# Two chained transformer blocks in fp32 on one core: block borders, the final layer norm and the first slots of each layer in a new order

## The reference, cut to what matters

```python
# first block, one layer (first_block)
hn = rms_norm(h, ln_pre_mix)
# projections, sliding-window and forgetting attention -> mix
h = h + rms_norm(mix @ w_out, ln_post_mix)
hn = rms_norm(h, ln_pre_ffn)
gu = hn @ w_gate_up                           # 1024 -> 2 * 2816
ff = (silu(gu[..., :D_FF]) * gu[..., D_FF:]) @ w_down
h = h + rms_norm(ff, ln_post_ffn)
# second block, two layers (hybrid_layer)
shift, scale, gate = split(silu(c) @ w_ada + b_ada)
u = x * (1 + scale) + shift
proj = u @ w_in                               # conv, gates, latents of q and kv, merge logits
# three branches, one of them latent attention -> m
x = layer_norm(DEEPNORM_ALPHA * x + gate * (m @ w_o), ln_g, ln_b)
```

## Time and profile before

| | us |
|---|---|
| median of 3 runs | 2003.44 (2001.84 to 2005.49) |
| the profiled execution's own time | 1998.23 |
| its span, first to last instruction | 1996.4 |
| TensorE busy with matmuls | 1818.6 |
| VectorE busy | 1068.3 |
| ScalarE busy | 703.0 |
| GpSimd busy | 129.9 |
| mean granted TensorE clock | 0.958 of full speed |

### The profile page before, as it was taken

The page is one execution under the profiler, slowest core; times in us unless marked ns, Lnnn a source line. Parts: engine busy times, 40 slices in busy tenths (PEclk is TensorE's granted clock), DMA queues, the critical chain, the costliest instruction groups (busy, mean ns, idle before and its releaser), DMA issues.

```text
span 1996.4 us, 20299 instructions
## 1 busy us (share of the span) xinstructions
PE 1818.6 (91%) x8139; PEld 1416.4 (71%) x8139; DVE 1068.3 (54%) x1694; ACT 703.0 (35%) x1131; POOL 129.9 (7%) x129
## 2 busy tenths in 40 slices
PE   4999999889999998989999999994889999999993
PEld 3765555568888787767778788773667778788772
DVE  6144444286666325563447867553453448866453
ACT  3324444342221223245532322423255532322422
POOL 1100000101010001000000000013000000000012
PEclk9899999799999999999989999997899999999996
DMA  3311000225555322121113222221121112232210
GB/s 131 131 66 41 22 22 22 74 95 211 180 209 183 114 104 106 63 85 64 64 43 104 86 94 96 85 92 56 64 85 64 64 43 105 85 106 85 98 71 42
DMA packets 29100, 177.40 MB, mean 89 GB/s; under 512 B 3565, under 2 KB 3709, under 8 KB 11726
## 3 DMA queue, kind: packets, MB, share of 16 engines
q1 hardware_dynamic: 20016, 144.71, 20.3%
q0 software_dynamic: 8608, 31.21, 4.6%
q10 hardware_dynamic: 382, 0.19, 0.1%
HBM read 171.28 MB, written 4.78 MB: 88 GB/s over the span
## 4 chain that ended last, share of the span: by engine, by line
PE 67%; DVE 7%; ACT 3%; POOL 1%; issue 1%; DMA 1%; POOLq 0%; ACTq 0%; DVEq 0%
PE ps L553 21%; PE ps L555 20%; PE ps L554 20%; PE ps L1006 2%; DVE w_lo L1462 2%; PE ps L991 2%; DVE R L1507 1%; ACT h L1053 1%; POOL acc L472 1%; ACT w_hi L1053 1%; PE ps L997 1%; PE ps L593 1%; DVE cacc L1469 0%; DMA w_raw<-in_w 0%; DVE ps L1824 0%
## 5 line engine op out<-in xcount | busy, mean ns | idle before, releaser
L553 PE MATMUL ps<-Xh,w_hi 128*128 128x512 f32 x1616 | 652.3, 404 | 55.7 <-DVE Xl L1462 26.2
L555 PE MATMUL ps<-Xh,w_lo 128*128 128x512 f32 x1616 | 636.5, 394 | 0.0
L554 PE MATMUL ps<-Xl,w_hi 128*128 128x512 f32 x1616 | 636.3, 394 | 0.0
L1462 DVE TENSOR_TENSOR w_lo<-w_raw,w_hi 128x2048 fp32r<-128x2048 f32 (+1 forms) x152 | 313.6, 2063 | 339.7 <-ACT w_hi L1053 339.7
L553 PEld LDWEIGHTS ps<-Xh,w_hi 128*128 128x128 f32 x1616 | 308.0, 191 | 132.7 <-issue 42.5
L1053 ACT ACTIVATE w_hi<-w_raw 128x2048 fp32r<-128x2048 f32 (+1 forms) x152 | 259.4, 1707 | 314.4 <-DMA w_raw<-in_w 282.5
L554 PEld LDWEIGHTS ps<-Xl,w_hi 128*128 128x128 f32 x1616 | 308.6, 191 | 65.9 <-issue 4.6
L555 PEld LDWEIGHTS ps<-Xh,w_lo 128*128 128x128 f32 x1616 | 307.7, 190 | 66.2
L1469 DVE SCALAR_TENSOR_TENSOR cacc<-ain,vec,cacc 128x512 f32<-128x512 f32 x240 | 161.9, 746 | 0.0
L1053 ACT ACTIVATE gt<-ps 128x512 f32<-128x512 f32 x48 | 28.2, 597 | 201.2 <-PE ps L555 201.1
L553 PE MATMUL ps<-act_h,w_hi 128*128 128x512 f32 x176 | 70.9, 403 | 4.3 <-DVE act_l L1462 4.3
(11 more groups left out here) (296 smaller groups left out, 2250.0 us busy)
## 6 DMA issues: line engine op xcount, KB each, us to landing
w_raw<-in_w SPq DMA_DIRECT2D x134, 1024.0 KB, 4.8
ada_w<-in_w_ada POOLq DMA_DIRECT2D x48, 512.0 KB, 4.6
bias_scratch<-brow POOLq DMA_DIRECT2D x2, 1312.0 KB, 5.3
h<-in_xT SPq DMA_DIRECT2D x4, 512.0 KB, 6.2
out<-h SPq DMA_DIRECT2D x1, 2048.0 KB, 6.3
bias<-bias_scratch POOLq DMA_DIRECT2D x1, 1024.0 KB, 7.6
bias<-bias_scratch POOLq DMA_DIRECT2D x1, 512.0 KB, 4.9
cact<-in_c POOLq DMA_DIRECT2D x1, 512.0 KB, 6.6
```

The source lines that it names most:

```text
L553: nc.tensor.matmul(o_, whi, xhi, start=start, stop=False)
L554: nc.tensor.matmul(o_, whi, xlo, start=False, stop=False)
L555: return nc.tensor.matmul(o_, wlo, xhi, start=False, stop=stop)
L1462: return nc.vector.tensor_tensor(o_, a_, b_, op)
```

## The change

Out projection: the first two tiles of slot 11 are computed together, k outermost (`window_step`), the first half of them ahead of the last attention values. Gate/up: `sums(2)` and the 128x512 reciprocal give way to `token_sums` and `spread` inside the last k-step of `two_slots`; ScalarE copies the spread result to `R`. `two_slots` waits for the second slot's `w_lo` by quarters. Down: the first four activation tiles are split during the last two gate/up slots, the output tiles are taken in another order at first with a wait for each bank, and the four late adaptive columns move between the down slots. End of down: VectorE adds the squares, ScalarE and VectorE share the copies to `y`, and the split of slot 47 is cut in quarters. Layer start: other banks, `sums(nsum)` between the two tiles of slot 2, slot 4's `slot_hi` ahead of the fifth latent and its `slot_lo` ahead of the latents. Layer end: after four of the eight output tiles their mean (of 512 channels) is taken off all 8 tiles of `h`; the true mean's difference to it (`delta`) and the variance are 128x4 sums at the end. Layer 1's input is made tile by tile with `lnp` (gain and bias merged with scale and shift); `h` itself stays without gain and bias, and the scaling by DEEPNORM_ALPHA in layer 1 adds them. The result is stored in four parts of 512 KB.

The diff, cut to its core, with eight columns of indentation less:

```diff
+EARLY = KD // 2
...
+LAT_BANK = (2, 3, 4, 5, 0, 6)
...
-    sp.wait_ge(ln_out, LAYERS * KD)
-    sp.dma_start(out, h[:, :, :]).then_inc(out_done, 16)
-    sp.wait_ge(out_done, 16)
+    for i in range(4):
+        sp.wait_ge(ln_out, 2 * i + 2)
+        sp.dma_start(out[:, 2 * i:2 * i + 2, :], h[:, 2 * i:2 * i + 2, :]).then_inc(out_done, 16)
...
-    add_early_squares(1, 1)
+    add_up(KD, 1, squares(0, KD - 1, KD))
+    pool.wait_ge(sum_full, 2)
+    pool.sem_inc(sq_added, 1)
...
-    add_early_squares(3, 2)
...
-        add_up(n + (5 + 2 * KC + KD), norm + 5, squares(0, KD, nsq + (5 + KC)))
+                for j in range(EARLY)])
+        add_up(n + (5 + 2 * KC + EARLY), norm + 5, squares(0, KD - 1, nsq + (5 + KC)))
+        pool.wait_ge(sum_full, norm + 6)
+        pool.sem_inc(sq_added, 1)
...
-    def two_slots(g, ready):
-        pe.wait_ge(w_lo_done, g + 2)
...
+        split_ready(g)
         for k in range(KD):
             pe.wait_ge(lo_done, ready + k + 1)
+            if norm is not None and k == KD - 1:
+                token_sums(norm, (norm + 1) * KD, (), B_ST)
             for i in range(4):
+                if i == 2:
+                    split_ready(g + 1, k // 2)
+                if norm is not None and k == KD - 1 and i == 3:
+                    spread(norm, B_O)
                 whi, wlo = w(g + i // 2, k * 2 * P + i % 2 * P)
-                last = mm3(bank(i), whi, wlo, Xh[:, k, :], Xl[:, k, :], k == 0, k == KD - 1)
+                last = mm3(bank(b0 + i), whi, wlo, Xh[:, k, :], Xl[:, k, :], k == 0, k == KD - 1)
...
+    def window_step(k):
+        pe.wait_ge(o_lo, 4 + k + 1)
+        for j in range(2):
...
+        if u == UNITS - 1:
+            split_ready(S_OW)
+            window_step(0)
+            window_step(1)
         values(u)
     assert done == DENSE_STEPS
+    window_step(2)
+    window_step(3)
...
+        for j in range(2 if g == S_OW else 0, 4):
...
-    sums(2, 3 * KD)
+    two_slots(S_GU, KD, 0, norm=2)
...
+    def down_bank(j):
+        if j in (0, 2):
+            pe.wait_ge(bank_read[0], fills.f[0].val())
+        if j == 1:
+            pe.wait_ge(bank_read[1], fills.f[1].val(-1))
+        if j in (6, 3):
+            pe.wait_ge(bank_read[1], fills.f[1].val())
...
-                for j in range(KD):
+                for j in (4, 5, 7, 0, 1, 2, 6, 3):
+                    if q == 0 and kk == 0:
+                        down_bank(j)
...
-    keep_busy(3, bank(B_O), T)
+    for b in range(2):
...
+    token_sums(3, 4 * KD - 2, (KD - 2, KD - 1), 0)
+    keep_busy(1, bank(1), T)
+    spread(3, 1)
+    keep_busy(3, bank(0), T)
...
-        two_slots(G, split0)
-        sums(nsum, nadd + 3)
-        pe.wait_ge(w_lo_done, G + 3)
+        two_slots(G, split0, 2)
...
-                last = mm3(bank(4 + j), whi, wlo, Xh[:, k, :], Xl[:, k, :], k == 0, k == KD - 1)
+                last = mm3(bank(LAT_BANK[4 + j]), whi, wlo, Xh[:, k, :], Xl[:, k, :], k == 0, k == KD - 1)
             last.then_inc(tile_full if j == 0 else slot_done, 1)
+            if j == 0:
+                sums(nsum, nadd + 3)
...
+                    if s == 0 and j == 0:
+                        pe.wait_ge(lo_done, split0 + (KD + 5 + 3 * KC + k + 1))
+                    if 2 * s + j == EARLY and k == KD - 3:
+                        sums(nsum + 4, nadd + (5 + 2 * KC + EARLY))
+                    whi, wlo = w(g, k * 2 * P + j * P)
+                    last = mm3(bank(j), whi, wlo, Xh[:, k, :], Xl[:, k, :], k == 0, k == KD - 1)
+                last.then_inc(tile_full if j == 0 else slot_done, 1)
...
+        pe.wait_ge(mean_added, 2 * L + 2)
+        pe.wait_ge(bank_read[0], fills.f[0].val())
+        block_sums(0, R, True)
+        pe.wait_ge(sq_added, nadd + (5 + 2 * KC + EARLY + KD - 1))
+        pe.wait_ge(rt_done, nsum + 5)
+        block_sums(2, acc, True)
+        pe.wait_ge(bank_read[1], fills.f[1].val())
+        block_sums(0, h[:, KD - 1, :], False, True).then_inc(mean_full, 1)
+        pe.wait_ge(sq_ready, SQ1 + SQUARES2 * L + SQUARES2)
+        block_sums(2, sq[:, (KD - 1) % 2, :], False, True).then_inc(sum_full, 1)
+        for i in range(2):
+            pe.wait_ge(diag_done, SPREADS1 + 2 * L + i + 1)
+            for t in range(NB):
+                last = nc.tensor.matmul(bank(B_O + i, P, c0=P * t), ones[:, :], tmp[:, i, t * P:(t + 1) * P],
+                                        start=True, stop=True)
+            last.then_inc(r_spread, 1)
+        if L + 1 < LAYERS:
+            keep_busy(3, bank(3), T)
...
-    root(2)
+    token_root(2, B_ST)
+    sc.wait_ge(r_spread, 2)
+    act_(R[:, :], bank(B_O), ACT.Copy).then_inc(r_copied, 1)
...
+        if t >= KF - 2:
+            down_hi(t - (KF - 2))
...
+    for q in range(1, KF // 2):
+        slot_hi(S_DOWN + q + 1)
+        if q > 1:
+            down_hi(q)
...
         square(bank(j), 3 * KD + j, j)
+        if j in (0, 2, 4):
+            y_copied = act_(y[:, j, :], bank(j), ACT.Identity, scale=vec1[:, 3 * KD + j:3 * KD + j + 1])
...
-    token_root(3, 4)
+    token_root(3, 0)
+    for j in (KD - 2, KD - 1):
+        act_(y[:, j, :], bank(j), ACT.Identity, scale=vec1[:, 3 * KD + j:3 * KD + j + 1]).then_inc(down_read, 1)
...
-                next_hi(3)
+                next_hi(L_CG)
+                next_hi(L_CG + 1)
...
-        next_hi(L_CG + 1)
...
-            act_(h[:, j, :], h[:, j, :], ACT.Copy, scale=DEEPNORM_ALPHA).then_inc(h_scaled, 1)
+            if L == 0:
+                act_(h[:, j, :], h[:, j, :], ACT.Copy, scale=DEEPNORM_ALPHA).then_inc(h_scaled, 1)
+            else:
+                act_(h[:, j, :], h[:, j, :], ACT.Identity, scale=lnp[:, 2, j:j + 1], bias=lnp[:, 3, j:j + 1]
...
+        act_(warm[:, :], eps[:, 0:1], ACT.Sqrt)
...
+        def centred_square(j):
+            if j < EARLY:
+                sc.wait_ge(zc_ready, (KC + EARLY) * L + (KC + j + 1))
+            else:
+                sc.wait_ge(bank_read[j % 2], FILL1[j % 2] + FILL2 * (L + 1) - 4 + j // 2 + 1)
+            square(h[:, j, :], nadd + (5 + 2 * KC + EARLY + j), j)
...
         for j in range(KD):
-            sc.wait_ge(zc_ready, (KC + KD) * L + (KC + j + 1))
-            square(h[:, j, :], nadd + (5 + 2 * KC + KD + j), j)
-        root(nsum + 5, 1)
...
+            centred_square(j)
+        sc.wait_ge(var_done, L + 1)
+        act_(rs[:, :], var[:, :], ACT.Sqrt, bias=eps[:, 1:2]).then_inc(rt_done, 1)
+        if L + 1 == LAYERS:
+            for j in range(KD):
+                sc.wait_ge(ln_mid, KC * LAYERS + j + 1)
+                act_(h[:, j, :], h[:, j, :], ACT.Identity, scale=vec(L, V_LG + j), bias=vec(L, V_LB + j)
+                     ).then_inc(ln_out, 1)
...
-    slot_lo(S_GU + 2)
-    inv_root(2)
-    ve.wait_ge(cact_done, 1)
+    for part in range(2):
+        slot_lo(S_GU + 2, part)
+    token_roots(2)
+    for part in range(2, 4):
+        slot_lo(S_GU + 2, part)
+    ve.wait_ge(r_copied, 1)
...
+        if t >= KF - 2:
+            down_lo(t - (KF - 2))
...
+        if t == 0:
+            ve.wait_ge(cact_done, 1)
...
+    for q in range(1, KF // 2):
+        slot_lo(S_DOWN + q + 1)
+        if q > 1:
+            down_lo(q)
+        if 2 <= q < 6:
+            c = 2 * KF + q - 2
+            ada_column(c, c // 2, c % 2, sgate[:, :, :].rearrange("p a n -> p (a n)"))
...
+    ln_g, ln_b = vec2[:, 0, V_LG:V_LG + KD], vec2[:, 0, V_LB:V_LB + KD]
+    ts(lnp[:, 2, :], ln_g, DEEPNORM_ALPHA, None, ALU.mult)
+    ts(lnp[:, 3, :], ln_b, DEEPNORM_ALPHA, None, ALU.mult)
+    tt(lnp[:, 0, :], ln_g, ada[:, 32:40], ALU.mult)
+    own.link(tt(lnp[:, 1, :], ln_b, ada[:, 32:40], ALU.mult))
+    own.link(tt(lnp[:, 1, :], lnp[:, 1, :], ada[:, 24:32], ALU.add))
...
+    for j in range(1, KD - 2):
...
+            tt(acc[:, :], acc[:, :], sq[:, j % 2, :], ALU.add).then_inc(sq_added, 1)
+        if j % 2:
+            y_copied = ts(y[:, j, :], bank(j), vec1[:, 3 * KD + j:3 * KD + j + 1], None, ALU.mult)
...
+    for part in range(2):
+        slot_lo(SLOTS1 + 1, part)
+    token_roots(3)
+    ve.wait_ge(r_spread, 3)
+    ve.sem_inc(sq_added, 2)
...
-        ve.wait_ge(sq_ready, 3 * KD + j + 1)
-        ts(y[:, j, :], bank(j), vec1[:, 3 * KD + j:3 * KD + j + 1], None, ALU.mult
...
+        if j >= KD - 2:
+            ve.wait_ge(down_read, j - (KD - 3))
+        own.link(tt(tmp[:, j % 2, :], y[:, j, :], bank(1), ALU.mult))
...
+        if 1 <= j < 3:
+            slot_lo(SLOTS1 + 1, j + 1)
...
-        if L:
-            next_lo(1)
-            split_input(lambda o_, j: ts(o_, h[:, j, :], ada_col(8 + j), ada_col(j), ALU.mult, ALU.add), split0)
...
+        next_lo(L_CG + 1)
         latents(nsum, 0, 3, V_QG)
-        next_lo(L_CG + 1)
...
+                jj = 2 * s + j
+                if jj == EARLY:
+                    ve.wait_ge(sum_full, nsum + 5)
+                    for t in range(KD):
+                        ins = stt(h[:, t, :], bank(B_ST), -1.0 / (EARLY * P), h[:, t, :], ALU.mult, ALU.add)
+                        if t < EARLY:
```

(45 more changed lines are left out.)

166 lines of the change are left out of this document (84 added, 82 removed).

## The result

The changed kernel takes 1940.79 us in the median of 4 runs (1937.73 to 1942.36), against 2002.85 for the kernel before on the same chip: a ratio of 0.9686, 95% interval 0.967 to 0.9703. The prediction said 1939 (1930 to 1956).

The account below looks back on a forecast made before the run. TensorE, busy 1818.6 of 1996.4 us, was taken to lose winnable time only at stage borders. Gains of 66.4 us less 0.4, 0.5 and 1.5 give 64.0, so 2003.44 becomes 1939.4; forecast 1939, range 1930 to 1956.

Parts of the forecast that it names:

- Out projection: Slot 11: last attention values' high part and rest come about 0.4 us late for the last k-step; 0.4 us lost.
- Start of gate/up: Third slot starts at 432.8 instead of 435.9, 3.1 us; short gap keeps full clock, 2.7 more; 5.8 us won.
- Start of down: The 4.26 us wait for the first activation rest goes, with about 2.8 us at lower clock; 7.1 us won.
- Moved ada columns: Inside down slots: four columns take idle VectorE time, but their loads meet weight loads; 0.5 us lost, bounds 0 and 3.
- Start of layer 0: A 2.8 us wait for a bank replaces the 4.5 us wait for `w_lo`; `L_UQ`'s third tile earlier; 7.8 us won.
- Rival B: New waits at borders bring the lower clock, layer starts end at lower bounds, down loses 2: 48 us won, 1955; chance 0.25.
- Between the layers: Layer 0's last dense product to layer 1's first: short norm tail, restart at 1382.2 instead of 1402.0; 19.8 us won.
- Inside layer 1: Scaling with gain and bias, 0.72 us instead of 0.53 times 8, loses 1.5; the moved sum loses 1.8.
- End: After the last dense product: spreads earlier, 512 KB store landing in 4.05 us, end at 1984.8; 11.6 us won.
- C: Rival: restart between the layers at full clock and less lost at layer starts, 72 us won, 1931; chance 0.04.
- D: Rival: clock falls at the new seam ahead of gate/up and stays low long; slower, 2019 with 400 matmuls; chance 0.02.
- E: Rival: no change, since the parts wait for each other at places not seen; chance 0.01.

Follow-up runs that it names:

- experiment 4: Changed kernel with slot 11's tiles in the old order and each layer's fourth and fifth slots split in the old order: 1943.95 us.
- experiments 7 to 9: Separate edits of the changed kernel: GpSimd's loads behind its additions, 1928.67 us; scalings of h in y slots, 1930.82; gate tile and a high part earlier, 1928.16.
- experiment 1: Changed kernel with the start of gate/up as before (sums(2) behind the first two slots, wide root and reciprocal): 1942.05 us.
- Experiment 2: Changed kernel with the first four activations again split behind gate/up and the output stored by one 2 MB transfer: 1949.05 us.
- experiment 3: Changed kernel with the last four ada columns again behind down and each layer's first sum again ahead of slot 2: 1955.64 us.
- experiment 6: Changed kernel with layer 1's eight scalings of h as Copy by one constant, without gain and bias: 1935.68 us.

## Why the prediction was right, point by point

- **Out projection** (0.4 lost): 0.9 by experiment 4. Within its bounds of 0 to 1. The wait of 6.1 us stayed, as said; its cause, GpSimd's queue, was named in the prediction, but what it would bring to remove it was not priced. It was 7.7 us, more than any other wait that experiments 7 to 9 took away.
- **Start of gate/up** (5.8): 5.3 by experiment 1. The new gap is 0.81 us (0.9 predicted) and the clock behind it is full in all 12 executions that have it.
- **Start of down** (7.1): wait gone, as said. Experiment 2 gives 6.0 in its execution, because 7 matmuls ran slow and not 13.
- **Moved ada columns** (0.5 lost, bounds 0 to 3): 0 by experiment 3. The four parts that the prediction names for the chain of a down slot add up to 9.2 us, not to the 10.5 that it states, so by its own numbers the slack was 2.0 us and not 0.7. Late, the columns would cost 8.2.
- **End of down** (8.1): 19.1 us became 10.7, so 8.4.
- **Start of layer 0** (7.8): 5.9 and 6.1. The wait is the one forecast (2.8 us, for the bank that ScalarE's gate activation frees). What failed is that the restart behind it was taken at full clock: five or six slow matmuls make 1.0 to 1.2 us, and the restart itself came 0.8 later. Rival B had this; it came true for these places.
- **Start of layer 1** (6.2): 4.7 with 13 slow matmuls, 7.3 with none. The number was between.
- **Between the layers** (19.8): 20.8 in the table. 13.2 us from the last product to the first, 13.5 predicted. The moved sum waited 0.77 us (0.9 predicted) and made the last eight tiles 2.0 us longer (45.27 us from their first product to their last, 43.29 before; 1.8 predicted). That is 20.0 us for the border itself; the other 0.8 was won further ahead, between `L_UQ` and the output slots of layer 0. The low clock at the restart comes about 2 us behind it, seven matmuls from 1358.2 on.
- **Inside layer 1** (3.3 lost, 1.5 for the scaling and 1.8 for the sum): 7.2 and 6.1. Mis-sized term: the scaling, 3.0 us by experiment 6, because the longer wait also brings the lower clock. Another 1.5 us is the low stretch near 1835, which the profiled execution of before happened not to have and layer 0 had in both kernels. With the moved sum's 2.0 us these make 6.5.
- **End** (13.4 with its own sum): 14.4. The landing was taken at 4.05 us from the rows of larger transfers and is 2.6, below the lower bound of 3.3. Against this the prediction's own terms end the eight tiles at 1980.2 (1969.5 and 8 times 1.34 us), not at 1979.6, so its 11.6 should have been 11.0. The estimate from the Trainium skill ("DMA: Bandwidth & Descriptors", section "Anatomy of one DMA"), 3.2 us, was nearer and still high; that section describes transfers issued by GpSimd, and this store is issued by SyncE. Its warning of late completions at HBM doesn't show here.

The sum, 64.0, was right within 2 us against the medians, partly by terms that balance: the end gave 1.0 more, between the layers 1.0 more, layer 0's start 1.8 less, layer 1's inside 3 to 4 less. It is also right by luck with the executions: the prediction would have the profiled execution at 1934.2, and it took 1941.05, 6.9 us more. Only because the profiled execution of before stood about 5 us below its median, and that of the changed kernel at its own, does the forecast of the median come out within 2 us.

Of the rivals B came true in part: the clock fell behind waits of 2.8 us, not behind the one of 0.8, and down lost nothing; it took far less than its 16 us. C, D and E did not come. The six signs that the prediction names for being right are all there. Of its signs for being wrong one is there in part: clock 0.54 behind layer 1's gate wait, though not behind the gate/up seam.

## What to carry to other kernels

Ask for each wait that stays what is queued ahead of the instruction that ends it: GpSimd's wait for slot 11, put with three loads ahead of the squares that it must add up, cost 7.7 us here, more than four of the seven parts of the change brought. Price a wait on TensorE of 2 us or more with the matmuls behind it, and look at a second execution before a difference of 3 us is put down to an edit. When a step is made longer by 0.2 us times eight, look whether its engine is the one being waited for.
